# Root of the second third ahead of the last load, and half a low part moved, around the gated unit of a two-layer decoder trunk

## The reference, cut to what matters

```python
def rms_norm(x, w):
    y = xf * lax.rsqrt(jnp.mean(xf * xf, axis=-1, keepdims=True) + EPS)
    return (y * w).astype(x.dtype)
# layer 1
    m = s5_mixer(hn, ...)          # ends: val, gate = split(y @ w_glu, 2); return val * sigmoid(gate)
    h = h + rms_norm(m, norm_mix_post[i])        # "post" norm, m = 0 below
    hn = rms_norm(h, norm_ffn_pre[i])            # "pre" norm, m = 1 below
    f = swiglu_ffn(hn, w_gate, w_up, w_down)     # 1024 -> 2816 -> 1024
```

## Time and profile before

| | |
|---|---|
| time, median of 3 runs (lowest, highest) | 2744.46 us (2744.45, 2746.97) |
| the profiled execution: its own time | 2745.94 us |
| the profiled execution: span of the profile | 2744.2 us |
| PE busy | 2669.0 us, 97% of the span |
| DVE, ACT, POOL busy | 1262.3, 625.6, 1029.9 us |
| granted TensorE clock, mean of the execution | 0.992 of full speed |

### The profile page before, as it was taken

How to read it: one execution, slowest core, us unless ns; L and a number is a source line. 1 busy time by engine, 2 the same in 40 slices (tenths; PEclk the granted TensorE clock), 3 DMA queues, 4 the chain that set the end, 5 groups by cost and what they waited for, 6 DMA issues and landing times.

```text
span 2744.2 us, 44629 instructions
## 1 busy us (share of the span) xinstructions
PE 2669.0 (97%) x18033; PEld 2549.3 (93%) x18033; DVE 1262.3 (46%) x2119; ACT 625.6 (23%) x1108; POOL 1029.9 (38%) x467
## 2 busy tenths in 40 slices
PE   8999999999999999999999999899999999999998
PEld 7999788866999999999999889799899999999997
DVE  5666567666174444444442456711632222222225
ACT  4231333365151000000000332411520000000002
POOL 5444110035354444444333425052544444444431
PEclk9999999999999999999999999999999999999999
DMA  4225322120232222222223139641331111111102
GB/s 163 93 108 142 92 63 63 37 80 25 82 112 69 76 82 82 82 75 82 76 82 96 52 117 281 219 126 32 108 108 46 46 46 46 46 46 46 46 31 82
DMA packets 142549, 232.25 MB, mean 85 GB/s; under 512 B 34016, under 2 KB 104928, under 8 KB 140256
## 3 DMA queue, kind: packets, MB, share of 16 engines
q1 hardware_dynamic: 53552, 134.98, 15.5%
q10 hardware_dynamic: 88880, 95.59, 10.9%
HBM read 172.78 MB, written 61.96 MB: 86 GB/s over the span
## 4 chain that ended last, share of the span: by engine, by line
PE 87%; DVE 6%; issue 2%; ACT 2%; DMA 1%; POOL 1%; ACTq 0%; DVEq 0%; POOLq 0%
PE psum L831 24%; PE psum L832 24%; PE psum L833 24%; PE psum L920 2%; PE psum L1323 2%; PE psum L1297 1%; DVE area L2310 1%; DVE area L2277 1%; PE psum L1145 1%; DVE x_lo L2322 1%; PE psum L1166 1%; PE psum L1415 1%; PE psum L1310 1%; DVE area L2300 1%; PE psum L1401 1%
## 5 line engine op out<-in xcount | busy, mean ns | idle before, releaser
L831 PE MATMUL psum<-x_hi,w_hi 128*128 128x344 f32 (+2 forms) x3456 | 1125.6, 326 | 0.7 <-issue 0.7
L832 PE MATMUL psum<-x_lo,w_hi 128*128 128x344 f32 (+2 forms) x3456 | 1106.9, 320 | 0.0
L833 PE MATMUL psum<-x_hi,w_lo 128*128 128x344 f32 (+2 forms) x3456 | 1106.3, 320 | 0.0
L770 POOL TENSOR_TENSOR w_hi<-stage,const 128x1024 fp32r<-128x1024 f32 x193 | 483.8, 2507 | 1484.9 <-PE psum L833 1315.3
L831 PEld LDWEIGHTS psum<-x_hi,w_hi 128*128 128x128 f32 x3456 | 651.2, 188 | 11.1 <-issue 3.7
L832 PEld LDWEIGHTS psum<-x_lo,w_hi 128*128 128x128 f32 x3456 | 651.3, 188 | 3.3 <-issue 1.7
L833 PEld LDWEIGHTS psum<-x_hi,w_lo 128*128 128x128 f32 x3456 | 650.6, 188 | 0.0
L773 POOL TENSOR_TENSOR w_lo<-stage,w_hi 128x1024 fp32r<-128x1024 f32 x193 | 486.3, 2520 | 15.1
L2782 DVE TENSOR_TENSOR area<-area,psum 128x344 f32<-128x344 f32 (+2 forms) x132 | 67.6, 512 | 652.9 <-ACT area L1999 652.9
L831 PE MATMUL psum<-act_hi,w_hi 128*128 128x344 f32 (+2 forms) x1056 | 341.8, 324 | 7.5 <-DVE area L2805 6.2
L833 PE MATMUL psum<-act_hi,w_lo 128*128 128x344 f32 (+2 forms) x1056 | 337.0, 319 | 0.0
(11 more groups left out here) (236 smaller groups left out, 2232.5 us busy)
## 6 DMA issues: line engine op xcount, KB each, us to landing
stage<-wstream SPq DMA_DIRECT2D x193, 512.0 KB, 3.5
s_set<-area ACTq DMA_DIRECT2D x8, 1600.0 KB, 7.2
proj<-area ACTq DMA_DIRECT2D x20, 520.0 KB, 2.7
area<-proj ACTq DMA_DIRECT2D x36, 256.0 KB, 3.7
resid<-area ACTq DMA_DIRECT2D x6, 1376.0 KB, 6.0
area<-resid ACTq DMA_DIRECT2D x6, 1376.0 KB, 10.0
area<-s SPq DMA_DIRECT2D x8, 1024.0 KB, 6.4
area<-proj ACTq DMA_DIRECT2D x12, 520.0 KB, 5.1
```

What stands on the lines that cost most here:

```text
L770: pool.tensor_tensor(per_block(w_hi[:, slot, :]), src, ones_block, ALU.mult).then_inc(high_split, 1)
L831: mm(out[:, 0:n], w_hi[:, slot, wk], hi[:, xk, a:a + n], start=first, stop=False)
L832: mm(out[:, 0:n], w_hi[:, slot, wk], lo[:, xk, a:a + n], start=False, stop=False)
L833: return mm(out[:, 0:n], w_lo[:, slot, wk], hi[:, xk, a:a + n], start=False, stop=last)
```

## The change

On ACT `norm_load(3, 2)` moves from ahead of `norm_root(3, 1, 0)` to behind `norm_square(3, 1, 1)`, directly ahead of `norm_store(3, 1)`. On DVE the loop over thirds 0 and 1 is written out, and the second half of `norm_low(3, 0)` moves from ahead of item 21's multiply to behind `norm_post(3, 1)`. Nothing is computed otherwise.

```diff
             norm_high(3, 0)
             glu_sigmoid((21,))
-            norm_load(3, 2)
             norm_root(3, 1, 0)
             glu_sigmoid((22,))
             norm_square(3, 1, 1)
+            norm_load(3, 2)
             norm_store(3, 1)
             glu_sigmoid((23,))
             norm_root(3, 1, 1)
...
             glu_product(range(18))
             square_fold(3, 0, 0)
-            for c in range(2):
-                glu_product((18 + 3 * c,))
-                norm_post(3, c)
-                glu_product((19 + 3 * c,))
-                square_fold(3, c, 1)
-                glu_product((20 + 3 * c,))
-                norm_pre(3, c)
-                square_fold(3, c + 1, 0)
-                if c == 0:
-                    norm_low(3, c)
+            glu_product((18,))
+            norm_post(3, 0)
+            glu_product((19,))
+            square_fold(3, 0, 1)
+            glu_product((20,))
+            norm_pre(3, 0)
+            square_fold(3, 1, 0)
+            norm_low(3, 0, (0,))
+            glu_product((21,))
+            norm_post(3, 1)
+            norm_low(3, 0, (1,))
+            glu_product((22,))
+            square_fold(3, 1, 1)
+            glu_product((23,))
+            norm_pre(3, 1)
+            square_fold(3, 2, 0)
             ffn(1, 3)
```

## The result

The changed kernel is slower: 2749.16 us median against 2745.22 us of before, 16 runs each; ratio 1.0016, 95% interval 1.0009 to 1.0023. The forecast of 2745.2 with a range up to 2748.0 missed it. The profiled execution spans 2748.4 us, 4.2 more than before, so it can be read for the whole difference.

What follows compares the result with a forecast made beforehand. PE was taken as the bound, busy 97% of the span, leaving only its waits to move. -1.95 at the first hole and +2.6 at the second gave +0.65 on 2744.46, about 2745.2 us; range 2741.8 to 2748.0.

Steps and rivals of the forecast that it cites:

- Steps 1 to 4: From root (3, 1, 0) through post norm, moved low part and fold: sum (3, 1, 1) starts about 1960.5, 1.95 us earlier.
- one turn behind POOL: On DVE, a two-input SBUF instruction waits for POOL's whole instruction: a low part takes 3.7 us instead of 1.6 free.
- first hole: PE's 5.5 us wait ahead of sum (3, 1, 1), plus 1.7 of fallen clock: 7.2 us, all there is to win.
- 1.6 + 2.1: Working for DVE and POOL taking turns: the two times add to 3.7 us on both sides.
- Step 5: ACT's load, store 0.6 us behind: store issued 1956.8, lands after 10.8 at 1967.6, bounds 1963.2 and 1969.3.
- the same situation: Profile row of two loads issued together, second landing after 10.8 us, taken as the store's landing time.
- step 4: DVE after the post norm: moved low part 3.7 us behind POOL, then item 22 and fold (3, 1, 1) until 1960.4.
- Step 6: DVE's norm_pre(3, 1) waits for the store until 1967.6; fold (3, 2, 0) behind it is done at 1974.5.
- second hole: New PE wait ahead of sum (3, 2, 0), predicted at 2.5 us, entered as +2.6 in the total.
- step 7: PE wants fold (3, 2, 0) at 1972.0; sum (3, 2, 0) starts at 1974.6 instead of 1973.96.
- slower: the second hole lets the clock fall again: Rival: PE's clock falls again, up to 1.7 us; with a slab-delayed store +2.3 to +4, 2746.8 to 2748.5; chance 0.25.
- The rule beside it: Trainium skill's DMA queue rule: a later descriptor may finish first, so a store need not stand behind a load.

Runs made afterwards that it cites:

- e9: Changed kernel with the last network's fifth and sixth slab loads held on SyncE until third 1's store landed; 2749.61 us, ratio 1.0020 to before.
- e10: e6 with the fifth and sixth slab loads held until third 1's low parts are made; 2742.46 us, ratio 0.9992 to before.
- e7: Changed kernel with the two transfers still issued together, but the store ahead of the load; 2742.99 us, ratio 0.9994 to before.
- e4: Kernel before with only the root (3, 1, 0) put ahead of the load, which stays right behind it; 2742.54 us, ratio 0.9997 to before.
- e3: Kernel before with only ScalarE's part of the change, both low parts left in place; 2749.03 us, ratio 1.0014 to before.
- e6: e2 with the moved half low part behind the fold (3, 1, 1) instead of ahead of it; 2740.87 us, ratio 0.9987 to before.
- e8: e6 with e5's own PSUM bank and early fold added; 2740.77 us, ratio 0.9989 to before.
- e2: Changed kernel with the load issued only behind the root (3, 1, 1), after the store; 2742.98 us, ratio 0.9994 to before.
- e1: Changed kernel with the store of third 1 issued ahead of the load of third 2; 2743.93 us, ratio 0.9995 to before.
- e5: Changed kernel with third 1's sums in their own PSUM bank and fold (3, 2, 0) ahead of the pre norm; 2745.94 us, ratio 1.0005 to before.

## Why the prediction was wrong

Steps 1 to 4 held to half a microsecond. The root was there at 1942.7 (predicted 1942.9), the post norm began at 1942.95 (1943.2), the moved low part was made at 1956.2 (1956.2) in one turn behind POOL, the sum (3, 1, 1) began at 1960.0 (1960.5) after the fall of the clock and took 3.98 instead of 4.23. The first hole shrank by 2.3 us, as against 1.95. (The 3.7 of a turn is right, its working "1.6 + 2.1" is not: the free split in the earlier trace rows took 2.42, and no row has 2.1. Nothing else hangs on it.)

**Step 5 failed in its size.** It took 10.8 us for the store from a pair without other traffic and let one slab at most into the upper bound, 12.5. The measured 13.8 lies beyond that bound. Two slabs were on the line: one issued at 1954.9, ahead of the load, and one at 1962.2, ahead of the store's end:

```profile
L694 SPq DMA_DIRECT2D stage<-wstream x1: 332/332/332, 1954.9 to 1954.9; - x1
...
DMA to landing us min/median/max: 3.6/3.6/3.6
...
L694 SPq DMA_DIRECT2D stage<-wstream x1: 332/332/332, 1962.2 to 1962.2; - x1
...
DMA to landing us min/median/max: 6.4/6.4/6.4
```

The price of the pair was right (e9 gives 10.7 once they are away), but it was not "the same situation": ahead of and among the pair in the earlier trace rows there was no slab until 1.2 us before its end. SP issues a slab when POOL is through a split, and step 4 had worked out POOL's pace, so both slabs could have been counted; 1.7 for each would have given 14.2, an estimate. The lower bound was read loosely too: the 6.4 of the earlier trace rows, called "alone", had the slab of the earlier trace rows beside it. With no slab near, the store took 5.6 (e10):

```profile
DMA to landing us min/median/max: 5.6/5.6/5.6
```

**Steps 6 and 7 were mis-sized.** The pre norm began 3.05 us later than predicted (1970.65 against 1967.6). Step 6 let the fold behind it wait for POOL until 1974.5; it took 1.58, with no turn, and ended at 1976.1. So the sum began 1.65 later than predicted, and as PE was there 0.6 earlier (1971.4 against 1972.0), the second hole was 4.85 instead of 2.6. The clock fell behind it, 1.7 us that step 7 and the sum put at nothing. The hole (2.25) and the clock (1.7) make 4.0 of the miss; the first hole gave back 0.4 more than forecast. The forecast left that fall to the rival "slower: the second hole lets the clock fall again", at 0.25, with +2.3 to +4. That rival is what happened (+4.2 in the spans, +3.9 in the medians): a rise of 0.16%, within the 5.5 us called no change, but clear of 1 over 16 runs. The sum took the price of the clock at its lower bound, nothing, though it could reach only upwards. The base was a part of the miss as well: the forecast stood on 2744.46, the median of three runs, and 16 runs give 2745.22. From that base the range would have ended at 2748.8, still below 2749.16.

**The rule beside it.** That a later transfer may finish its write first did not show: with the load first the store landed 4.6 + 0.6 us behind it, with the store first 6 us ahead of it (e7). Between two queues no such order held: the slab that SP issued at 1962.2, 5.4 us behind the store, landed at 1968.6, 2.0 us ahead of it. The Trainium skill, DMA: Bandwidth & Descriptors, section Queues, rings and completion order, also says that descriptors are consumed in ring order on each DMA engine; that part agrees with the landings of ACT's queue.

**Where the gain went.** The whole 7.2 us hung on one relay, and the change moved a transfer that the relay needs later (the store) behind one that nobody needed soon (the load). The root ahead of the load shortens the first hole by 2.4 us (e4), though its gain in time is not clear of noise; the load ahead of the store costs all of the loss (e3); and the half low part is worth nothing where it was put (3.19 against e3's 3.07) and the rest of the first hole where it could have been put (e6).

Open: why the clock stayed low longer after some holes than after others of the same length, why it fell behind some and not behind others (e6, e8), and what order of slabs and low parts would let e6 keep the 4.2 us that B takes back.

## What to carry to other kernels

Of two transfers on one queue, the one that somebody waits for goes ahead of the one that nobody waits for soon: the 1376 KB ahead of the store cost 5.1 us here (10.7 in e9 against 5.6 in e10, both without slabs), and the two slabs of 512 KB from the other queue 3.1 more (13.8 against 10.7). When work is moved off a chain, look whether it lands ahead of the chain's last link or behind it; only behind it counts. And when two engines take turns, as DVE and POOL do here, moving the work of one of them can move the turns to the next chain that needs the other (e10).

## What the runs showed of the hardware

- The granted clock after a hole of 3.1 to 3.2 us was low for different times in the same code: back at 1963.4 in e2, at 1965.25 in e1, with holes that ended at 1960.56 and 1959.41. The sum behind it took 3.96 and 4.92 us. Two profiles can so differ by about 1.5 us of the clock alone; whether two executions of one kernel do was not looked at.
- The clock can fall after the hole: in the changed kernel PE stood from 1971.4 to 1976.25, and the fall came at 1976.5. It can also fall sooner: in e5 PE stopped at 1954.2, and the clock fell at 1956.2.
- Two transfers of 1376 KB issued 0.6 us apart on one queue landed by order of issue, whichever of them reads memory: store then load 6.8 and 12.3 us, load then store 9.2 and 13.8, each time with one slab issued 1.2 or 1.3 us ahead and one on the way; load then store 7.4 and 10.7 without slabs.
- A store of 1376 KB with no other transfer near took 5.6 us (e10), with a slab ahead of it or beside it 6.3 to 6.8 (before, e1, e2, e4, e6, e7, e8).
